# A two-layer trunk's first norm: x turned as it lands, the norm's row applied as a column scale, first products ordered by weight halves

## What is computed

```
h    = x * rsqrt(mean(x*x) + eps) * g        # g: one row of 1024, the norm's gain
proj = h @ w_in                              # w_in: 1024 x 6224, 4096 gate columns, then u,v | q,k,v | latents | a,g
```

## Time and profile before

| | |
|---|---|
| median of 3 runs | 1017.18 us (1016.47 to 1017.36) |
| the profiled execution's own time | 1017.16 us |
| its span in the profile | 1015.3 us |
| TensorE busy | 1002.2 us, 99% of the span |
| VectorE, ScalarE busy | 811.8 us (80%), 649.9 us (64%) |
| chain that ended last | PE 89%, DVE 5%, ACT 3%, DMA 2% |

### The profile page before, as it was taken

One profiled execution on the slowest core, in us unless ns is written; L12 is line 12 of the kernel. 1 busy time (PEld: TensorE's weight loads), 2 busy tenths in 40 slices (PEclk: granted clock), 3 DMA queues, 4 the chain that ended last, 5 costly groups with the idle time before them and its releaser, 6 DMA issues.

```text
span 1015.3 us, 13999 instructions
## 1 busy us (share of the span) xinstructions
PE 1002.2 (99%) x4930; PEld 846.9 (83%) x4930; DVE 811.8 (80%) x1112; ACT 649.9 (64%) x890; POOL 38.4 (4%) x87
## 2 busy tenths in 40 slices
PE   7999999999999999999999999999999999999998
PEld 6888888888888888888888888888888988898887
DVE  5799888765544455699889768999889989989898
ACT  6658655555534443756674548787778787868775
POOL 6000000040000000100000000000000000000020
PEclk9999999999999999999999999999999999999999
DMA  9735555677555554844555556999999999999995
GB/s 272 240 122 168 172 179 168 209 241 248 169 195 188 195 177 129 289 147 133 178 172 181 189 190 217 323 379 389 365 340 393 384 364 346 390 369 362 358 395 204
DMA packets 117701, 257.13 MB, mean 253 GB/s; under 512 B 5217, under 2 KB 29859, under 8 KB 117649
## 3 DMA queue, kind: packets, MB, share of 16 engines
q1 hardware_dynamic: 113344, 243.55, 68.8%
q0 software_dynamic: 3296, 9.22, 3.3%
q10 hardware_dynamic: 1008, 3.67, 0.9%
HBM read 249.08 MB, written 7.34 MB: 253 GB/s over the span
## 4 chain that ended last, share of the span: by engine, by line
PE 89%; DVE 5%; ACT 3%; DMA 2%; issue 1%; SPq 0%; DVEq 0%; ACTq 0%
PE bank L390 27%; PE bank L392 27%; PE bank L391 27%; DMA ring<-in_w_in 2%; DVE wlo L378 1%; ACT whi L371 1%; PE bank L1082 1%; DVE dacc L1719 1%; PE bank L1005 1%; PE bank L1004 1%; PE bank L674 1%; DMA ring<-in_moe_w_gate 1%; PE bank L664 1%; PE bank L908 0%; PE bank L689 0%
## 5 line engine op out<-in xcount | busy, mean ns | idle before, releaser
L378 DVE TENSOR_TENSOR wlo<-ring,whi 128x1024 fp32r<-128x1024 f32 (+2 forms) x506 | 541.4, 1122 | 102.2 <-ACT whi L371 99.9
L371 ACT CAST whi<-ring 128x1024 fp32r<-128x1024 f32 (+2 forms) x506 | 463.4, 971 | 97.0 <-PE bank L392 79.1
L390 PE MATMUL bank<-whi,hTh 128*128 128x512 f32 (+3 forms) x992 | 375.4, 378 | 2.0 <-DVE wlo L378 1.3
L392 PE MATMUL bank<-whi,hTl 128*128 128x512 f32 (+3 forms) x992 | 370.4, 373 | 0.0
L391 PE MATMUL bank<-wlo,hTh 128*128 128x512 f32 (+3 forms) x992 | 370.1, 373 | 0.0
L390 PEld LDWEIGHTS bank<-whi,hTh 128*128 128x128 f32 x992 | 186.4, 188 | 32.4 <-issue 2.7
L392 PEld LDWEIGHTS bank<-whi,hTl 128*128 128x128 f32 x992 | 186.3, 188 | 29.1
L391 PEld LDWEIGHTS bank<-wlo,hTh 128*128 128x128 f32 x992 | 186.5, 188 | 28.4 <-issue 0.5
L390 PE MATMUL bank<-whi,oTh 128*128 128x512 f32 x392 | 155.4, 396 | 0.0
L392 PE MATMUL bank<-whi,oTl 128*128 128x512 f32 x392 | 153.1, 391 | 0.0
L391 PE MATMUL bank<-wlo,oTh 128*128 128x512 f32 x392 | 152.9, 390 | 0.0
(11 more groups left out here) (333 smaller groups left out, 672.4 us busy)
## 6 DMA issues: line engine op xcount, KB each, us to landing
ring<-in_w_in SPq DMA_DIRECT2D x40, 1024.0 KB, 5.2
ring<-in_moe_w_down SPq DMA_DIRECT2D x40, 1024.0 KB, 7.5
ring<-in_moe_w_gate SPq DMA_DIRECT2D x32, 1024.0 KB, 7.3
ring<-in_moe_w_up SPq DMA_DIRECT2D x32, 1024.0 KB, 8.2
ring<-in_moe_w_gate SPq DMA_DIRECT2D x16, 768.0 KB
ring<-in_moe_w_up SPq DMA_DIRECT2D x16, 768.0 KB, 7.4
ring<-in_ffn_w_gate SPq DMA_DIRECT2D x11, 1024.0 KB, 5.1
ring<-in_ffn_w_up SPq DMA_DIRECT2D x11, 1024.0 KB, 5.2
```

Source lines behind the costliest of these rows:

```text
L371: nc.scalar.copy(whi[pc.part(hf)][:, 0:n], pc.raw[:, hf * n:(hf + 1) * n]).then_inc(hi_done, 1)
L378: nc.vector.tensor_tensor(wlo[q][:, 0:n], pc.raw[:, hf * n:(hf + 1) * n], whi[q][:, 0:n].bitcast(F32), ALU.subtract).then_inc(lo_done, 1)
L390: nc.tensor.matmul(o, sh, wh, start=start, stop=False)
L392: return nc.tensor.matmul(o, sl, wh, start=False, stop=stop)
```

## The change

**Transfers.** x comes in four column halves of 256 KB: the first 512 columns of both tiles, then piece 0 in two halves of 512 KB, then the last 512 columns of both tiles, then piece 1 and so on. The broadcast of the gain is gone; ScalarE's queue loads it as an 8 x 128 block (4 KB). GpSimd builds `ident` first, before it issues the positions; its 17 parameter transfers start when piece 1 has landed, in a new order, and are counted by two semaphores: five early ones (`early_in`) and twelve others (`param_in`).

**The norm.** x itself is turned, not x*g. TensorE turns the 8 x 128 gain block into a column (`gcol`, one value per partition and k block), and g goes in as a scale by partition: in the cast of the turned tokens (`first_upper`, ScalarE, eight of 256 columns) and in the low part (`first_lower`, VectorE, (turned x * g) - high, eight of 256 columns). The four multiplications of x by g are gone, and so are L1158's and L1484's four passes each.

**The products.** Chunk 0 goes by pairs of k blocks: for each, four high*high products, four low tokens * high weights, and last four high tokens * low weights, each group behind its own wait. The turns of x's second half (`turned_x(2)`, `turned_x(3)`, eight transposes) lie behind the first pair's products. The idle products are 4 and 4 in place of 4 and 6, on `ident` alone, and start with `ident_ready`.

**The angles.** VectorE makes them in the mixer's step 0, behind the low parts of piece 2; sine and cosine move to ScalarE's step 1, behind the casts of piece 3 and ahead of chunk 0's eviction.

In the second layer the counts of semaphores change, and the order of the parameter transfers.

The diff, cut to its core:

```diff
-
-            eng.wait_ge(raw_in[pc.slot], pc.landed)
-            for hf in range(2):
+        def split_hi(eng, pc, n=HALF, halves=(0, 1)):
+
+            if pc.first == 0 and halves[0] == 0:
+                eng.wait_ge(first_in, 16)
+            else:
+                eng.wait_ge(raw_in[pc.slot], pc.landed)
+            for hf in halves:
                 if pc.first >= PARTS // 2:
                     eng.wait_ge(w_used, 2 * pc.number + hf + 1 - PARTS)
                 nc.scalar.copy(whi[pc.part(hf)][:, 0:n], pc.raw[:, hf * n:(hf + 1) * n]).then_inc(hi_done, 1)
...
         def _(sp):
-            sp.dma_start(x[:, 0, :], a['x'][0, 0:P, :]).then_inc(x_in[0], 16)
-            sp.dma_start(gain[:, :], a['attn_norm'][0:1, :].to_broadcast([P, D])).then_inc(gain0_in, 16)
-            sp.dma_start(x[:, 1, :], a['x'][0, P:2 * P, :]).then_inc(x_in[1], 16)
+            def first_half(hf):
+                dst = Piece(0).raw[:, hf * HALF:(hf + 1) * HALF].rearrange("p (k c) -> p k c", c=512)
+                w = a['w_in'][0].rearrange("(k p) n -> p k n", p=P)
+                c0 = GATES + CHUNKS[0][0]
+                return sp.dma_start(dst, w[:, 2 * hf:2 * hf + 2, c0:c0 + 512])
+
+            def x_half(g):
+                for m in range(MT):
+                    cols = slice(512 * g, 512 * (g + 1))
+                    sp.dma_start(x[:, m, cols], a['x'][0, P * m:P * (m + 1), cols]).then_inc(x_in[m][g], 16)
+
+            x_half(0)
+            first_half(0).then_inc(first_in, 16)
+            first_half(1).then_inc(raw_in[Piece(0).slot], 16)
+            x_half(1)
...
                 for ci, (c0, n) in enumerate(CHUNKS):
                     for part in range(2):
+                        if l == 0 and ci == 0 and part == 0:
+                            continue
                         fetch(pcs[2 * ci + part], w[:, 4 * part:4 * part + 4, GATES + c0:GATES + c0 + n], 4, n)
...
-            def row(dst, src, slow=False):
-                pool.dma_start(dst, src, allow_slow_non_contiguous=slow).then_inc(param_in, 16)
+            def early(dst, src, slow=False):
+                pool.dma_start(dst, src, allow_slow_non_contiguous=slow).then_inc(early_in, 16)
+
+            def row(dst, src):
+                pool.dma_start(dst, src, allow_slow_non_contiguous=True).then_inc(param_in, 16)
...
+                early(cwr[0:D_CONV, :], a['d_conv_w'][l])
+                early(wsr[:, :, :], a['a_ws'][l].rearrange("g t s -> t g s"))
+                early(dcol[:, 0, :], a['d_conv_b'][l].rearrange("(c p) -> p c", p=P), slow=True)
+                early(cngain[:, 0:CQ], vec('c_cq_norm').to_broadcast([P, CQ]))
+                early(cngain[:, CQ:CQ + CKV], vec('c_ckv_norm').to_broadcast([P, CKV]))
                 row(uq[:, 0, :], a['c_w_uq'][l, 0:P, :])
...
             nc.gpsimd.memset(ident[:, :], 0.0).then_inc(pool_seq, 1)
+            pool.wait_ge(pool_seq, 1)
+            nc.gpsimd.affine_select(out=ident[:, :], in_=ident[:, :], compare_op=ALU.not_equal, fill=1.0, base=0,
+                                    pattern=[[-1, P]], channel_multiplier=1).then_inc(ident_ready, 1)
+            pool.dma_start(posi[:, :], a['positions'][0].rearrange("(m p) -> p m", p=P),
+                           allow_slow_non_contiguous=True).then_inc(pos_in, 16)
...
-            pool.wait_ge(raw_in[Piece(0).slot], Piece(0).landed)
+            pool.wait_ge(raw_in[Piece(1).slot], Piece(1).landed)
             load_params(0)
...
+            def turned_x(pair):
+                for m in range(MT):
+                    pe.wait_ge(x_in[m][pair // 2], 16)
+                    for i in range(2):
+                        k = 2 * pair + i
+                        last = nc.tensor.transpose(bank[4 + pair][:, T * i + P * m:T * i + P * (m + 1)],
+                                                   x[:, m, P * k:P * (k + 1)], ident[:, :])
+                last.then_inc(hT_mm, 1)
...
-                pe.wait_ge(param_in, 16 * N_PARAM * (l + 1))
+                pe.wait_ge(early_in, 16 * N_EARLY * (l + 1))
...
                 pe.wait_ge(cnT_ev, l + 1)
                 pe.wait_ge(wprep_ev, l + 1)
+                pe.wait_ge(param_in, 16 * N_PARAM * (l + 1))
...
+                def first_columns():
+                    tiles = [slice(P * m, P * (m + 1)) for m in range(MT)]
+                    for pair in range(4):
+                        pc, hf = Piece(pair // 2), pair % 2
+                        wh, wl = (w[pc.part(hf)][:, 0:1024].rearrange("p (k c) -> p k c", c=512) for w in (whi, wlo))
+                        ks = (2 * pair, 2 * pair + 1)
+                        pe.wait_ge(hi_done, pair + 1)
+                        pe.wait_ge(hT_hi, pair + 1)
+                        for k in ks:
+                            for m, t in enumerate(tiles):
+                                nc.tensor.matmul(bank[m][:, :], hTh[:, k, t], wh[:, k % 2, :], start=(k == 0),
+                                                 stop=False)
+                        pe.wait_ge(hT_lo, pair + 1)
+                        for k in ks:
+                            for m, t in enumerate(tiles):
+                                nc.tensor.matmul(bank[m][:, :], hTl[:, k, t], wh[:, k % 2, :], start=False, stop=False)
+                        pe.wait_ge(lo_done, pair + 1)
+                        for k in ks:
+                            for m, t in enumerate(tiles):
+                                last = nc.tensor.matmul(bank[m][:, :], hTh[:, k, t], wl[:, k % 2, :], start=False,
+                                                        stop=(k == KD - 1))
+                        last.then_inc(w_used, 1)
+                        if pair == 0:
+                            turned_x(2)
+                            turned_x(3)
...
                     for part in range(2):
                         if ci == 0 and l == 0:
-                            pe.wait_ge(hT_lo, 2 * part + 2)
+                            if part == 0:
+                                first_columns()
+                            continue
...
-            pe.wait_ge(const_ready, 1)
+            pe.wait_ge(ident_ready, 1)
             idle_products(4)
-            transposed_h(0)
-            idle_products(6)
+            pe.wait_ge(gain0_in, 16)
+            nc.tensor.transpose(bank[2][:, 0:KD], gain[0:KD, 0:P], ident[0:KD, 0:KD]).then_inc(gcol_mm, 1)
+            turned_x(0)
+            turned_x(1)
+            idle_products(4)
             mixer(0)
...
+            def first_upper(pair):
+                act_e.wait_ge(hT_mm, pair + 1)
+                for i in range(2):
+                    k = 2 * pair + i
+                    last = nc.scalar.mul(hTh[:, k, :], bank[4 + pair][:, T * i:T * (i + 1)], gcol[:, k:k + 1])
+                last.then_inc(hT_hi, 1)
+
             def token_norm(k, piece=None):
 
                 if k == 0:
-                    norm_upper(k, 0, 2)
-                    split_hi(act_e, Piece(0), piece_half(0))
-                    norm_upper(k, 2, 2)
+                    act_e.wait_ge(gcol_ready, 1)
+                    first_upper(0)
+                    first_upper(1)
+                    split_hi(act_e, Piece(0), piece_half(0), (0,))
+                    split_hi(act_e, Piece(0), piece_half(0), (1,))
+                    first_upper(2)
+                    first_upper(3)
                     split_hi(act_e, Piece(1), piece_half(1))
+                    act_e.wait_ge(const_ready, 1)
                     link(square_sum(k, 0))
                 else:
                     act_e.wait_ge(x_new, 4 * (k - 1) + 2)
@@ -1257,6 +1336,10 @@
                         split_hi(act_e, pcs[s + 2], piece_half(s + 2))
                     elif s + 2 == MIX_PIECES:
                         split_hi(act_e, after_mixer(l, 0))
+                    if s == 1 and l == 0:
+                        act_e.wait_ge(ang_ready, 2)
+                        nc.scalar.activation(sinT[:, :, :], sinT[:, :, :], ACT.Sin)
+                        nc.scalar.activation(cosT[:, :, :], cosT[:, :, :], ACT.Sin).then_inc(trig_ready, 1)
...
-            act_e.wait_ge(const_ready, 1)
-            nc.scalar.copy(stat[:, 63:64], eps[:, :])
+            act_e.dma_start(gain[0:KD, 0:P], a['attn_norm'][0].rearrange("(k p) -> k p", p=P)).then_inc(gain0_in, 16)
+            act_e.wait_ge(ident_ready, 1)
+            nc.scalar.copy(stat[:, 63:64], ident[:, 0:1])
             token_norm(0)
-            act_e.wait_ge(ang_ready, 2)
-            nc.scalar.activation(sinT[:, :, :], sinT[:, :, :], ACT.Sin)
-            nc.scalar.activation(cosT[:, :, :], cosT[:, :, :], ACT.Sin).then_inc(trig_ready, 1)
             mixer(0)
...
+            def first_lower(pair):
+                dve.wait_ge(hT_hi, pair + 1)
+                for i in range(2):
+                    k = 2 * pair + i
+                    last = V.scalar_tensor_tensor(out=hTl[:, k, :], in0=bank[4 + pair][:, T * i:T * (i + 1)],
```

(29 more changed lines are left out.)

45 lines of the change are left out of this document (19 added, 26 removed).

## The result

The changed kernel takes 1019.73 us (median of 8 runs, 1018.79 to 1021.11), the kernel before 1016.97 beside it (8 runs, 1016.25 to 1017.44): ratio 1.0027, 95% interval 1.0017 to 1.0036. It is slower by 2.8 us, where 1013.4 was forecast. The profiled execution took 1020.64 us with a span of 1018.8, 3.5 us more than before on both counts (0.9 us above its own median).

A forecast was written before the change was run, and what follows sets the result against it. TensorE, busy 1002.2 of 1015.3 us, bounds the kernel. 4.9 - 0.9 - 0.6 - 0.4 + 0.4 = 3.4 us at chunk 2, 3.8 through VectorE at 74 us: 1017.16 - 3.8 = 1013.4, range 1012.6 to 1014.6, chance 0.65.

The forecast's parts named there:

- First product at 8.1: Start of TensorE's products: first one at 8.1 us instead of 12.96, 4.9 us earlier, with ScalarE last to be waited for.
- the curve of landings: First transfers: 0.5 MB landed at 4.5 us, 1.0 MB at 6.35, 1.5 MB at about 7.7, read from the earlier trace.
- B: Front: clock rises late, seven or eight first products at half clock cost 1.8 us, 1015.2; chance 0.11.
- D: Front: x halves or gain block land at 6.35 for 4.5, first product 1.9 us later, about 1015.2; chance 0.05.
- The chances of the three outcomes: Against no change: forecast and half of B and D 0.74; A and half of B and D 0.20; C 0.06.
- rival A: Piece 4's transfer again takes 13.5 us, landing at 30.0; TensorE only 1.2 us earlier at chunk 2, 1016.0; chance 0.13.
- Chunk 1 at 20.5: Chunk 1's start: root at 19.0 us, then a cast of 0.7 and low part of 0.83, giving 20.5.
- The stall behind it: Within chunk 1: TensorE wants piece 3 at 24.4 us, VectorE's low part ends at 24.8, a stall of 0.4.
- Chunk 2 at 30.0: Chunk 2's start: TensorE ready at 30.0 us without waiting, against 33.38 before, 3.4 us earlier.
- latent turns 3.8 earlier: At 74 us, where TensorE waits for VectorE: VectorE is 3.8 us earlier, so TensorE gains 3.8.
- The parameters, asked for when piece 1 has landed: Parameter transfers start at 11.8 us for 10.5; first needed at 28.7, so no cost even at 13.5 us of transfer.
- Rival C: Front: clock rises only after two pairs, 24 products and eight turns slow, 6.3 us; about 1018.7; chance 0.06.

The follow-up runs named there:

- e8: Changed kernel with the positions' 1 KB transfer issued only after piece 0's first half has landed: 1018.32 us, ratio 1.0017 to the kernel before.
- e16: Changed kernel with 12 idle products for 4 and the positions' transfer late, parameters left as changed: 1018.69 us, ratio 1.0015.
- e13: Changed kernel with 7 idle products in TensorE's wait ahead of the latent queries' turns at 75 us: 1019.04 us, ratio 1.0015.
- e5: Changed kernel with only the four narrow broadcasts held until piece 5 has landed: 1015.57 us, ratio 0.999.
- e10: Changed kernel with 12 idle products for 4, last six parameters held until piece 5 has landed, and positions late: 1013.23 us, ratio 0.9966.
- e1: Changed kernel with the 17 parameter transfers in the old order, still behind piece 1: 1019.1 us, ratio 1.0021.
- e4: Kernel before with the parameter transfers in the new order and nothing else: 1015.64 us, ratio 0.9992.
- The square: Four kernels, front as changed or repaired (12 idle products, positions late): parameters as changed 1019.73 and 1018.69 us; six behind piece 5, 1015.42 and 1013.23.
- e12: Changed kernel with 12 idle products, six parameters behind piece 5 and positions late, but angles, sine and cosine back ahead of the mixer's loop: 1017.84 us.

## Why the prediction was wrong, step by step

**First product at 8.1.** It came at 9.16. ScalarE was the last to be waited for, as forecast, and its scaled casts (1.57 for four, 1.7 forecast) started at 5.17 (5.4). The step that failed is the curve of landings, 0.5 MB at 4.5 us and 1.0 MB at 6.35. x's first halves were in time (TensorE turned them from 3.78 us and waited for neither), but piece 0's first half landed at 8.04 for 6.35, the second at 10.0 for 7.7, piece 1 at 14.1 for 11.8. The sum read that curve from whole tiles of x and the gain, and had nothing for x in halves of 2 KB rows and the positions' 4-byte transfer beside them (issued at 1.80 us); with the positions later (e8) the first product started at 8.26.

**Rivals B and D.** B's effect happened, not its mechanism. It was priced at 1.8 us with seven or eight slow products; twelve products lost 1.7. But the rise that it feared to be late had come at 5.7 us, where the idle records went from 0.26 to 0.13 us apart; what cost was a fall behind 2.4 us of standing. My reason for counting nothing was the time from TensorE's first work to the first product, and I had no term for an idle stretch between them. D did not happen: x's halves and the gain block were there in time (scaled casts from 5.17), and the 1.06 us came with piece 0. The chances of the three outcomes are also mis-added by 0.01: forecast and half of B and D is 0.73, A and half of B and D 0.21.

The Trainium skill ("TensorE: Matmul & The Clock Gate", Part 4) has turns in transpose mode not bring the full clock. In this kernel the first stretch of work was four idle products, then nine turns, and the fast rate came right behind the turns, so the start does not settle it. Nor do the falls: waits of 1.89 and 1.88 us with sixteen turns behind them (changed kernel, e16) were followed by 0.50, while one of 1.97 us with products behind it (chunk 2 in e13) left the granted clock at 1.00, which would fit; but at the front of e5 1.82 us of standing with products behind was followed by 0.50 too. Idle products on the identity in the wait at 75 us (e13) kept the clock; that is shown.

**Chunk 1 at 20.5.** 23.14 in the changed kernel, 20.97 in e10 (root 19.02 for 19.0 forecast). The stall behind it was 0.35 for 0.6. ScalarE's squares and root indeed did not move (15.36 in e10, 15.27 in the earlier trace rows).

**Chunk 2 at 30.0, latent turns 3.8 earlier.** 32.66 and 2.16 later in the changed kernel; 30.00 and 3.66 earlier in e10. The arithmetic from the front to chunk 2 held once its inputs were true.

**The parameters, asked for when piece 1 has landed: "no cost".** This is the step that decided. I asked when the parameters are needed, not what they do to others on their way. They were asked for 3.6 us later (14.37 for 10.79), in an order that puts the four narrow broadcasts near the end, from 21 to 23 us, and so upon piece 5, issued at 23.91. The order alone is not it: e1 with the old one is as slow, e4 with the new one behind piece 0 is not. With the four out of piece 5's way (e5) 4.2 us come back. I had looked for the late transfer (rival A), but at piece 4: issued at 19.1 for 16.5, 11.1 us under way for 9, it landed at 30.2 for 25.5, near A's 30.0, with 0.45 us of waiting; piece 5 had no term at all. The rows that would have shown it were in the trace of before: there the same broadcasts, issued at 10.8 to 12.5 us, were followed by a stretch of 14 to 18 us in which the transfers moved 89 GB/s, while no engine waited for one. The square prices the step at 4.3 to 5.5 of the 6.3 us between forecast and result, and the front at 1.0 to 2.2.

**Rival C** (1018.7, slower by the clock at the front) came nearest to the time, for the wrong reason: the slow products cost 1.7 us and not the 5.5 us or so of 24 of them, and e10's front, with no slow product, is worth 2.2 us with the parameters out of the way and some 1.0 (e16) without.

## What to carry to other kernels

When a change shifts a list of small transfers in time, ask which large transfer it lands on, or holds up on its way, and not only when its data are needed: look up how long its packets take, find in the trace before where the mean rate falls while they are in flight, and see who will be waiting there. A gain at the front reaches the end only through the last chain that can still be late; here that was piece 5's cast and VectorE behind it, and the start of the turns at 75 us foretold the medians of this study to 1 us (median less start of the turns lies from 941.6 to 943.3 in all with that start in the table but e8, 944.1). Price each idle stretch of TensorE with its clock: waits of 1.9 to 2.4 us cost 1 to 1.7 more behind them, though one of 1.97 us cost nothing.

## What the runs showed of the hardware that was not expected

- Broadcasts of narrow rows hold the transfer engines out of proportion. At 26 to 31 us of the changed kernel, 53 packets of 2048 and 3072 bytes of the GpSimd queue took 41 us of the engines' time, 0.98 and 0.50 us each, against 0.10 for the weights' packets of 2048 bytes, and the mean rate fell to 127 GB/s; in the kernel before, at 14 to 18 us, 28 such packets of 2048 bytes took 1.26 us each and the rate was 89. The Trainium skill ("DMA: Bandwidth & Descriptors", Why small descriptors are slow) names a fixed cost of some 3 cycles for each packet, 27% for a descriptor of 256 bytes. The trace has 0.98 us against 0.10 for the same 2048 bytes, so that cost does not explain it. Whether it is the narrow rows or that 128 of them are read from one place in memory, no run separates.
- A transfer of 1 KB in 4-byte elements at 1.8 us slowed the weights at 6 to 8 us from 358 to 226 GB/s (e8 against the changed kernel, and no overlap between the eight profiles with it early and the six with it late). Its own packets took 5% of the engines' time at 4 to 8 us; by what way it holds up the others stays open, all the more since the kernel before issued it at 1.36 us and still moved 395 GB/s at 6 to 8 us, with x in whole tiles.
- The granted clock fell after 2.41 us of idleness at the front (0.54 in the next microsecond), and after 3.29 us in e12, where it stayed at 0.50 for 4 us and more under full products. At the front it fell with 1.82 us (e5) and not with 1.70 (e1), at chunk 2 not with 1.97 (e13): the length of the wait alone does not decide.
